# Layer-1 adaLN rows moved from the first mixer to the second, parameter rows spread by a product with ones, adaLN bias as columns, S5 transposes at a later step

## What is computed

```
c_act = silu(c)
for l in range(2):
    mod = c_act @ ada_w[l] + ada_b[l]                   # 1024 -> 6 x 1024
    sh1, sc1, g1, sh2, sc2, g2 = split(mod, 6)
    h = rms_norm(x) * (1 + sc1) + sh1
    y = even_mixer(h) if l == 0 else odd_mixer(h)
    x = x + g1 * y
    h = rms_norm(x) * (1 + sc2) + sh2
    x = x + g2 * hier_moe(h)                            # 32 experts of 1024 x 512, top 2 of one group
```

## Time and profile before

| | us |
|---|---|
| median of 3 runs | 1529.42 (1528.27 to 1533.06) |
| the profiled execution | 1528.45 |
| its span, first to last instruction | 1526.7 |
| TensorE busy | 1366.4 (90%) |
| VectorE busy | 471.2 (31%) |
| ScalarE busy | 215.8 (14%) |
| GpSimd busy | 110.7 (7%) |
| the chain that ended last: TensorE / VectorE / DMA | 83% / 8% / 4% |

### The profile page before, as it was taken

One profiled execution on the slowest core, in us unless ns is written; L12 is line 12 of the kernel. 1 busy time (PEld: TensorE's weight loads), 2 busy tenths in 40 slices (PEclk: granted clock), 3 DMA queues, 4 the chain that ended last, 5 costly groups with the idle time before them and its releaser, 6 DMA issues.

```text
span 1526.7 us, 15421 instructions
## 1 busy us (share of the span) xinstructions
PE 1366.4 (90%) x6416; PEld 695.9 (46%) x6416; DVE 471.2 (31%) x874; ACT 215.8 (14%) x454; POOL 110.7 (7%) x98
## 2 busy tenths in 40 slices
PE   5399988789999999999995676978999999999997
PEld 2244445654444445444444234864454444445443
DVE  2144546432221212112113886253121221221112
ACT  1022243011111111111110004210010110101010
POOL 1300000300220220211200000000000000000000
PEclk8699999889999999999998888779999999999999
DMA  9997597319999999999996008114999999999993
GB/s 309 209 364 297 200 418 294 110 73 408 424 428 429 426 429 427 428 427 428 429 370 269 28 0 330 54 58 181 425 422 420 424 422 426 419 426 427 419 426 146
DMA packets 53021, 498.07 MB, mean 326 GB/s; under 512 B 4692, under 2 KB 5836, under 8 KB 21972
## 3 DMA queue, kind: packets, MB, share of 16 engines
q1 hardware_dynamic: 48960, 490.42, 77.7%
q0 software_dynamic: 1056, 1.30, 1.7%
q10 hardware_dynamic: 2932, 5.30, 0.9%
HBM read 491.76 MB, written 5.24 MB: 326 GB/s over the span
## 4 chain that ended last, share of the span: by engine, by line
PE 83%; DVE 8%; DMA 4%; ACT 2%; issue 2%; POOL 0%; DVEq 0%; SPq 0%; ACTq 0%; PEldq 0%
PE B L710 30%; PE B L727 15%; PE B L696 8%; PE A L737 7%; PE B L556 6%; PE A L638 4%; PE B L519 3%; PE B L717 2%; DMA ring<-in_ada_w 2%; DMA work<-in_s_c_im 2%; PE B L569 1%; PE B L504 1%; PE B L907 1%; DVE work L1403 1%; PE B L665 1%
## 5 line engine op out<-in xcount | busy, mean ns | idle before, releaser
L710 PE MATMUL B<-ring,work 128*64 128x512 f32 x2048 | 453.6, 595 | 14.3 <-DVE work L1189 12.5
L710 PEld LDWEIGHTS B<-ring,work 128*64 128x64 f32 x2048 | 142.3, 137 | 291.3 <-issue 272.4
L727 PE MATMUL B<-ring,work 128*64 128x512 f32 x1024 | 231.5, 594 | 1.2 <-ACT work L1547 1.2
L1193 DVE TENSOR_TENSOR work<-work,B 64x512 f32<-64x512 f32 x64 | 68.3, 1067 | 426.3 <-ACT work L1543 425.8
L727 PEld LDWEIGHTS B<-ring,work 128*64 128x64 f32 x1024 | 73.0, 137 | 140.1 <-issue 140.1
L1543 ACT ACTIVATE work<-B 64x512 f32<-64x512 f32 x64 | 37.7, 589 | 659.5 <-PE B L710 659.5
L696 PE MATMUL B<-work,htok 128*128 128x256 f32 x512 | 123.6, 387 | 6.7 <-issue 6.7
L1189 DVE COPY work<-B 128x512 f32<-128x512 f32 x80 | 55.3, 692 | 227.6 <-PE B L701 121.3
L737 PE MATMUL A<-work 128*128 128x256 f32 x512 | 116.2, 380 | 2.6 <-DVE work L1199 2.6
L737 PEld LDWEIGHTS A<-work 128*128 128x128 f32 x512 | 96.8, 190 | 18.1 <-issue 5.2
L696 PEld LDWEIGHTS B<-work,htok 128*128 128x128 f32 x512 | 95.1, 195 | 18.0 <-issue 6.8
(11 more groups left out here) (218 smaller groups left out, 931.9 us busy)
## 6 DMA issues: line engine op xcount, KB each, us to landing
ring<-in_moe_w SPq DMA_DIRECT2D x192, 2048.0 KB, 15.3
ring<-in_ada_w SPq DMA_DIRECT2D x24, 2048.0 KB, 17.1
ring<-in_ev_w_in SPq DMA_DIRECT2D x6, 2048.0 KB, 11.1
ring<-in_od_w_in SPq DMA_DIRECT2D x4, 2048.0 KB, 21.8
ring<-in_ev_w_out SPq DMA_DIRECT2D x2, 2048.0 KB, 13.7
s_tables<-hT ACTq DMA_DIRECT2D x16, 256.0 KB, 9.7
ring<-s_tables SPq DMA_DIRECT2D x2, 2048.0 KB, 11.1
ring<-in_od_w_out SPq DMA_DIRECT2D x2, 2048.0 KB, 11.2
```

What stands on the lines that cost most here:

```text
L710: ins = pe.matmul(B5[64 * m:64 * m + 64, :], xgT[:, g, k, CH * j:CH * j + CH], w[:, k, :], start=(k == 0), stop=(k == KD - 1))
L727: ins = pe.matmul(B7[64 * m:64 * m + 64, :], hidTb[:, q % 2, k, :], w[:, k, 512 * m:512 * m + 512], start=(k == 0), stop=(k == KF - 1))
L1193: dve.tensor_tensor(hid[64:128, q % 2, :].rearrange("p (k q) -> p q k", k=KF), silu_a[64:128, q % 2, :].rearrange("p (q k) -> p q k", k=KF ...
```

## The change

- `LOADS0` loses eight loads, ("ada", 1, 4) to ("ada", 1, 11); they stand in `LOADS1` between the projections' weights. The adaLN rows 1/1 and 1/2 are computed in the second mixer: rows 1/1 in two halves, after `project1(1)` and after `s5_output(2)`, rows 1/2 after `project1(5)`, in the transposes' banks. The first attention has no adaLN rows left. ScalarE copies them in its fixed list: r1 and c1 before the last z, r2, c2 and then `root(9)` behind it. `project1` takes its chunks in the order (0,0), (0,1), (1,0), (1,1), (2,0), (2,1).
- The twelve gain rows are loaded as rows on one partition (`prow`); two products with a row of ones (`parameter_rows`) put them on all partitions, and VectorE copies them to `prm`.
- The bias is loaded as 96 rows of 128, transposed once ("bias") to `modb`, and VectorE adds it to `modc` (`add_bias`); 1 is added to the scales' bias, so `modp` falls away. The bias matmuls are gone.
- "lam" is transposed after adaLN rows 0/1 (q == 1), bt and ct at q == 4; ScalarE's copies and activations move with them. `LATE_PARAMS` wait for `z_ready` 6.

```diff
@@ loads
-          + [("ada", 1, j) for j in range(12)] + [("out", 1), ("out", 0)])
-LOADS1 = [("in", 0), ("tab", 0), ("tab", 1)] + [("in", q) for q in range(1, 4)] + [("glu",), ("out", 1), ("out", 0)]
+          + [("ada", 1, j) for j in range(4)] + [("out", 1), ("out", 0)])
+LOADS1 = ([("in", 0), ("tab", 0), ("tab", 1), ("in", 1)] + [("ada", 1, j) for j in (4, 5)] + [("in", 2)]
+          + [("ada", 1, j) for j in (6, 7)] + [("in", 3)] + [("ada", 1, j) for j in range(8, 12)]
+          + [("glu",), ("out", 1), ("out", 0)])
@@ TensorE
-                    if k == 0:
-                        for g in range(4):
-                            pe.matmul(bank[32 * g:32 * g + 32, :], ident[:, 12 * l + 4 * r + g:12 * l + 4 * r + g + 1].to_broadcast([P, 32]),
-                                      brow[:, :], start=True, stop=False)
+            def parameter_rows():
+
+                pe.wait_ge(in_par, 16 * N_PAR)
+                for b in range(2):
+                    w = min(512, PROWS - 512 * b)
+                    ins = pe.matmul(A4[:, b, 0:w], ones[0:1, :], prow[:, 512 * b:512 * b + w], start=True, stop=True)
+                ins.then_inc(par_rows, 1)
...
+            tr_unit("bias", [brow[:, :]], [(in_brow, 16)])
+            parameter_rows()
             pe.wait_ge(c_ready, 1)
             ada_rows(0, 0)
...
-                if q == 0:
-                    tr_unit("lam", [s5row[:, :]], [(in_s5, 16 * N_S5)])
                 if q == 1:
                     ada_rows(0, 1)
+                    tr_unit("lam", [s5row[:, :]], [(in_s5, 16 * N_S5)])
...
             s5_input(0)
             project1(0)
-            for q4 in range(1, 4):
-                s5_input(q4)
-                s5_output(q4 - 1)
-                project1(q4)
+            s5_input(1)
+            s5_output(0)
+            project1(1)
+            bank = pass_bank("ada1r1")
+            ada_part(bank, 1, 1, range(0, 4))
+            s5_input(2)
+            s5_output(1)
+            project1(2)
+            project1(3)
+            s5_input(3)
+            s5_output(2)
+            ada_part(bank, 1, 1, range(4, KD))
+            pe.nop().then_inc(tr_done, 1)
+            pe.nop().then_inc(slot_used, 1)
             project1(4)
+            ada_columns(1, 1)
             s5_output(3)
             project1(5)
+            ada_rows(1, 2)
+            ada_columns(1, 2)
@@ VectorE
+            def add_bias(l, lo, hi, done):
+
+                dve.wait_ge(tr_ev, U[done] + 1)
+                tt(modc[:, l, lo:hi], modc[:, l, lo:hi], modb[:, l, lo:hi], ALU.add)
...
             for b in range(4):
                 square(b)
+            dve.wait_ge(tr_ev, U["bias"] + 1)
+            up = modb[:, :, :].rearrange("p l (w c) -> p (l w) c", w=2)[:, :, 8:16]
+            ts(up, up, 1.0, None, ALU.add)
+            dve.wait_ge(par_rows, 1)
+            dve.tensor_copy(prm[:, 0:512], A4[:, 0, :])
+            link(dve.tensor_copy(prm[:, 512:PROWS], A4[:, 1, 0:PROWS - 512]))
+            tell(par_ready)
             norm_modulate(0)
@@ ScalarE
                 if m == 5:
-                    root(9, small[:, 0:16])
+                    ada_evac(1, "r1")
+                    ada_evac(1, "c1")
                 act.wait_ge(proj_done, 19 + m)
                 act.copy(z1[:, t, 512 * ch:512 * ch + 512], B5[:, :]).then_inc(z_ready, 1)
+            ada_evac(1, "r2")
+            ada_evac(1, "c2")
+            root(9, small[:, 0:16])
@@ GpSimd
-            for dst, src, slow in PARAMS:
-                pool.dma_start(dst, src, allow_slow_non_contiguous=slow).then_inc(in_par, 16)
+            at = 0
+            for name, w in PARAMS:
+                pool.dma_start(prow[:, at:at + w], a[name][0:1, :]).then_inc(in_par, 16)
+                at += w
...
+            pool.wait_ge(z_ready, 6)
             for dst, src, slow in LATE_PARAMS:
```

128 lines of the change are left out of this document (58 added, 70 removed).

## The result

| | before | after |
|---|---|---|
| median, us | 1530.9 (1528.27 to 1533.06) | 1542.55 (1540.46 to 1544.43, 5 runs) |
| ratio | | 1.0074, 95% interval 1.0053 to 1.0095 |
| span of the profiled execution | 1526.7 | 1541.2 |
| TensorE busy | 1366.4 | 1368.7 |

The changed kernel is 0.74% slower, 11.7 us by the medians and 14.5 us by the two profiled executions. The prediction said 1545 and slower. TensorE is busy for 2.3 us more, so most of the time is in waits. In the rows of after, the adaLN products are L517, every transpose L506, `project0` L560, `project1` L573, ScalarE's `root` L1522, the S5 product that frees the tables L1434, the gate of S5 L944.

A forecast was written before the change was run, and what follows sets the result against it. The prediction saw full DMA engines in both MoE layers, waits for loads and S5 parameters in the opening, and VectorE pacing the attention. Second mixer +44 and first mixer -27.7 gave +16.3 on 1528.45, so 1545 us, range 1531 to 1559.

The forecast's parts named there:

- Parameter rows: Opening: twelve spread transfers become one-row ones, so the first projection starts at 36.5 instead of 43.46: -7 us, bounds -3 and -9.
- S5 parameters: First mixer: the wait moves behind the second projection and adaLN rows 0/1, loads are waited for instead: -7.4 us, bounds -3 and -14.
- VectorE's chain: First mixer: VectorE's S5 chain starts later but sinks into two idle times of VectorE: 0 us, at most +3.
- bias: First mixer, after the third projection: two sets of bias matmuls leave the straight work: -1.7 us.
- sums: First mixer: VectorE's added bias sums and the three on norms, which replace one behind the root: -0.6 us together.
- First attention: First layer's attention: 128 adaLN matmuls leave it and VectorE's waits for scores shrink: -11 us, bounds -7 and -12.7.
- Second mixer: ada6, ada7 and in3 wait for the tables' slots, root(9) and the first head norm behind them: +44 us, bounds +40 and +48.
- T: Second mixer: end of the last S5 quad (prod_ready 8), when a table's ring slot comes free; 915.9 before the change.
- the second attention has nothing to give back: Second attention: glu and output weights land by T + 51, before they are asked for, so nothing is regained.
- the moved work is hidden: Rival, second mixer: moved loads and products fit beside VectorE's S5 work, cost 0, time 1501; chance 0.07.
- The first mixer gives little: Rival: rows -3, S5 parameters -3, attention -7, first mixer -15; with +44 the time is 1557; chance 0.18.
- A gain of both ends: Rival: loads recover sooner (-14), rows give -9, first mixer -38; with +40 the time is 1531; chance 0.08.

The follow-up runs named there:

- ada_undo: Changed kernel with the eight adaLN loads and rows 1/1 and 1/2 back in the first mixer and its attention, without bias matmuls: 1506.99 us, ratio 0.9843.
- tabs_late_root: root_early with the S5 tables loaded fifth and sixth in the second mixer instead of second and third: 1514.1 us, ratio 0.9913.
- four_slots: Changed kernel with hand-given ring slots so only output weights take the tables' slots, project1(5) ahead of s5_output(3), root(9) ahead of r2 and c2: 1510.66 us.
- par_undo: Changed kernel with the gain rows spread over 128 partitions by twelve transfers again, products with ones and VectorE copies left out: 1551.56 us, ratio 1.0131.
- lam_undo: Changed kernel with the S5 eigenvalues' transpose and ScalarE's copy and exponential behind it at q == 0 again: 1549.63 us, ratio 1.0138.
- late_undo: Changed kernel with the late parameters issued right behind the S5 parameters, not waiting for z_ready 6: 1546.34 us, ratio 1.0092.
- root_early: Changed kernel with ScalarE taking root(9) before the fifth z copy instead of behind r2 and c2: 1536.35 us, ratio 1.0035.
- filler: Changed kernel with 16 unread TensorE products added in each of steps 1 to 7 of the first attention: 1545.83 us, ratio 1.0087.
- logdt_row: Changed kernel with the S5 log step loaded as one row of 32 behind the gain rows, replacing two strided spread transfers: 1527.91 us, ratio 0.9971.
- ada_undo_logdt: ada_undo with the S5 log step loaded as a row, as in logdt_row: 1493.3 us, ratio 0.9739.

## Why the prediction was right, step by step

The time, 1542.55, lies 2.5 us under the forecast, the direction is as forecast, and the mechanism that carried the sum (ada6, ada7 and in3 behind the tables, the first head norm behind them) is what ada_undo, tabs_late_root and four_slots show. The size is partly luck: the first mixer gave 21.0 us and not 27.7, the second cost 34.8 and not 44, and the two misses, 6.7 and 9.2 us, mostly cancelled.

- **Parameter rows, -7**: the first projection moved by -7.1, par_undo brings it back. The value was read from the bytes that didn't fit, and that way of reading held.
- **S5 parameters, -7.4**: -9.1. The step "where the parameters were waited for, loads are waited for" held: 22.04 us became 12.97, and lam_undo and late_undo split it into the moved wait and 2 us of late parameters. But I took the starvation as given and asked only where its wait would stand. Its own cause was worth more, 14.6 us of time and 18 to 20 up to MoE 0, than any term of the change in the first mixer.
- **VectorE's chain, 0; bias -1.7; sums -0.6**: the stretch from the third projection to the first score is 1.5 us longer, not 2.3 shorter. The third projection itself took 16.85 us instead of 13.97, at a granted clock that had fallen in the waits for loads; that is 2.9 of the 3.8 us. The chain sank into VectorE's idle times as said, the one of 10.13 us is 2.63 now. About 0.9 us remain unexplained. The bias was not tried by itself.
- **First attention, -11**: -7.8, the largest miss of one term in the first mixer but for the stretch above. I costed the removed products and the waits they caused, and took the remaining ones at their durations of before. They are not a constant: the same products took 40.6 us instead of 27.8. At the highest mean clock seen with this code the term would be 53.5 - 42.4 = 11.1, by the comparison in the section on the clock.
- **Second mixer, +44**: root(9) ran at T + 44.8, not + 47; the landings came as read (first adaLN product at T + 7.6, projection 4 at T + 18.0, said 18.9), the pieces of ScalarE and TensorE behind them took 2 us less than I gave them. The delay at the gate was 40.5. The last step, "the second attention has nothing to give back", stands: the stretch behind the gate was 4.0 us shorter in this execution (1.7 up to the output projection, 2.1 in it, 14.03 instead of 16.11 us), but that came with a higher granted clock, as the two windows under the table show, and not with the change. T came 1.7 us sooner after the mixer's start. Sum: +34.8, of which 4.0 are luck.
- The statement that only root(9) held the head norm was too simple: root_early shows that the root was worth 4 us beyond what TensorE's own queue holds.
- The upper bound was added up wrongly. With +3 of VectorE's chain and +2 of the late parameters among the terms it is 1566, not 1562; the lower one is 1530.5. The measured time lies inside either.

Of the rivals, *the moved work is hidden* is the one that four_slots makes true by hand, at the point named for it (ada6, ada7 and in3 landing before T). *The first mixer gives little* didn't come; the first mixer gave 21.0 up to MoE 0. *A gain of both ends* came nearest from the other side: the second mixer cost even less than its +40, the first gave less than its -38.

## What to carry to other kernels

A load moved within a ring doesn't stand where the list shows it but where the slot it takes comes free: write out whose slot it takes before costing anything else. Where a queue is starved, look at the share of time of each queue beside its bytes before taking the starvation as given; the smallest transfers can be the ones that do it. And work taken off an engine can make what stays slower: price what stays by a second row, not only what goes.

## What the runs showed of the hardware

- Two transfers of 4 KB each, with a strided last dimension and spread over 64 partitions, held the ring to between 17 and 126 GB/s for 16 us and made a 128 KB transfer issued beside them take 27.4 instead of 9.5 us. Two strided ones of 2 KB that are not spread left 247 GB/s.
- The granted clock fell to 0.50 in the first attention and stayed there for 20 us with TensorE shown busy; the attention's products took 40.6 us instead of 27.8. In filler, with 112 products (224 instructions) added, it stayed at 1.00 up to 216 us and the same products took 31.5 us.
- The mixer with the late loads is also the less steady one: kernels that differ only in the first mixer took 233.2 (lam_undo), 233.3 (after), 236.1 (filler), 236.6 (par_undo), 239.7 (logdt_row) and 239.8 us (late_undo) from `project1(0)` to MoE 1. With the old order of loads it was 198.4 (before), 198.7 (ada_undo) and 198.7 (ada_undo_logdt).
